# Which four experts a mixture-of-experts loop computes first, and its first and last step written out

## The chip, the cores and the metric

One core of one Trainium2 chip runs the whole program. The time is device microseconds (us) from the first to the last instruction and what lies around them, a median over runs; smaller is better.

## What is computed

One denoising step of a two-layer model on two samples of 128 tokens (sample 0 is the prompt, sample 1 the latent tokens), 1024 wide, float32. Each layer has a mixer and then a mixture of 32 experts. Only the second half of a layer matters here:

```python
g_idx = argmax(hf @ rg_w + rg_b)                     # one of 4 groups
top_v, top_i = top_k(e_logits of that group, 2)      # two of its 8 experts
w_sel = softmax(g_logits)[g_idx] * softmax(top_v)
hid = silu(einsum('nd,edf->nef', hf, w_gate)) * einsum('nd,edf->nef', hf, w_up)     # f = 256
out = einsum('nef,efd->nd', hid * gates, w_down)
```

The two samples make 512 picks of an expert in each layer, and the picks are uneven. Worked out from the reference's router and its inputs, the experts with picks are (expert: picks of sample 0 + picks of sample 1):

- layer 0: 0: 35+56, 1: 13+20, 2: 46+2, 3: 32+15, 4: 22+29, 5: 1+3, 6: 14+10, 7: 61+73, 8: 1+0, 9: 1+0, 24: 10+8, 25: 4+12, 26: 2+3, 27: 1+1, 28: 0+13, 29: 1+2, 30: 11+7, 31: 1+2
- layer 1: 8: 30+37, 9: 29+16, 10: 45+112, 11: 46+52, 12: 12+3, 13: 1+2, 14: 60+9, 15: 1+3, 16: 2+0, 17: 0+2, 18: 0+3, 19: 1+5, 20: 1+4, 24: 1+1, 25: 1+3, 26: 2+0, 27: 3+1, 28: 7+3, 30: 8+0, 31: 6+0

## The kernel before

An expert's picks are cut into chunks of 32 tokens. TensorE works on four columns of 32 at once, so one **step** of the expert loop computes four chunks, one in each column, and each column holds the weights of one expert: 6144 elements on each of 128 partitions, in three parts of 2048, the first and second half of the gate and up weights (`gu0`, `gu1`) and the down weights (`down`), 1024 KB each. A chunk plan made on the chip gives layer 0 seven steps (28 chunks) and layer 1 eight (32 chunks).

SyncE (SP) loads the weights into the columns, with one buffer for each column: in its own loop (L680 to L692) it reads the experts of the next step and a flag `fresh` for each column from the small table `meta`, waits until TensorE is done with the part (`gu0_done`, `gu1_done`, `down`), and issues the four loads of it; a column whose expert stays (`fresh` 0) moves nothing. The first step's weights are loaded earlier: as soon as sample 0 is routed, `first_keys`, `first_ranks` and `first_experts` on VectorE (DVE) rank the experts by the picks of sample 0 and take the **four least picked** (ranks 0 to 3 among those with a pick), and SP issues their twelve loads while sample 1 is still in its norm and router. Every chunk that is left then goes into the columns in the order of the experts, column after column, and `meta` is signalled when both samples are routed. In a step TensorE (PE) does, in this order:

- gate and up, `gu0` then `gu1` (L1282, 64 matmuls)
- the gather of the next step's tokens, as a product with a one-hot matrix (L1247)
- two times two transposes, of the gates (L1295) and of the hidden values (L1298)
- the scatter of the step before into four sums in PSUM (L1258); in step 0 it adds zeros
- down (L1310)

ScalarE (ACT) takes the exponential, copies `tH` and `tG`, and the first half of the output; DVE makes the hidden values (L2442 to L2448), the gates and the next selection. After the loop the last scatter follows (L1319). PE, ACT and DVE each wait for `meta` and read the number of steps before step 0. GpSimd (POOL) waits for the end of the down product of step 1 (`down` at 6, L781) and then loads the gate rows and norm weights for the end of the layer: two loads of 512 KB and one of 1024 KB, on the second DMA queue (q0), while SP's go through q1.

Of the kernel before, what the change touches and what calls it, by code (L numbers as in the profile page):

```python
# [15 lines left out]
ALU = mybir.AluOpType  # L16
# [3 lines left out]
P = 128  # L20
# [3 lines left out]
NS = 2  # L24
# [38 lines left out]
NCST = C_G4 + 64  # L63


def constants():
# [22 lines left out]
    c[:, C_M8:C_M8 + 8] = np.arange(8) - 1000.0  # L89
    return c  # L90
# [97 lines left out]
def build(nc, a, o):  # L188
# [41 lines left out]
    small = view(region(320), 320)  # L230
# [19 lines left out]
    BK2 = Banks(ps, [6], S("filled_side"), {"dve": S("drained_side")})  # L250
# [184 lines left out]
    def plan_first(l):  # L435
# [5 lines left out]
        for kind in ("first", "ranked", "early"):  # L441
            BK.add((kind, l), "dve")
# [3 lines left out]
    def plan_moe(l):  # L446
# [9 lines left out]
        for kind in ("base", "eid"):  # L456
            BK2.add((kind, l), "dve")
# [150 lines left out]
    R_EID, R_F, R_RF, R_F4 = 952, 1004, 1036, 1068  # L608
    R_FLAG, R_D = R_ZERO, R_ZERO + 64
# [24 lines left out]
    def _(sp):  # L634
# [26 lines left out]
        for l in range(2):  # L661
# [17 lines left out]
            steps = sp.value_load(meta[0:1, 0, 0:1], min_val=MINS, max_val=MAXT)  # L679
            with sp.Fori(1, steps) as it:  # L680
# [5 lines left out]
                for h in range(2):  # L686
                    sp.wait_ge(S(f"gu{h}_done{l}"), it + 1)
                    for c in range(NC):
                        load(f"gu{h}", *GU[h], c, expert[c], cond=fresh[c])
                sp.wait_ge(S(f"down{l}"), it * 2 + 2)  # L690
# [21 lines left out]
    def _(pool):  # L712
# [63 lines left out]
        for l in range(2):  # L776
# [4 lines left out]
            pool.wait_ge(S(f"down{l}"), 6)  # L781
# [20 lines left out]
    def _(pe):  # L802
# [376 lines left out]
        def first_rows(l):  # L1179
# [3 lines left out]
            pe.matmul(bank[0:1, 0:NC], cst[0:32, C_COL:C_COL + 1], rt_[0:32, R_F4:R_F4 + NC], start=True, stop=True)  # L1183
            pe.matmul(bank[:, 32:64], rt_[0:32, R_NB:R_NB + P], ident[0:32, 0:32], start=True, stop=True)
            pe.matmul(bank[:, 64:96], rt_[0:32, R_ZERO:R_ZERO + P], ident[0:32, 0:32], start=True, stop=True)\
                .then_inc(filled, 1)

# [10 lines left out]
        first_rows(0)  # L1198
        project_out(0, 1, 1, range(7, KT))


        def moe(l):
# [5 lines left out]
            filled_side = S("filled_side")  # L1208
            rows(l, 0)
# [20 lines left out]
            side_free("base")  # L1230
            pe.wait_ge(S("nchunks"), l + 1)
            bank, nb = side("base"), rt_[0:32, R_NB:R_NB + P]
            pe.matmul(bank[:, 0:32], nb, SU[0:32, 0:32], start=True, stop=True)
            pe.matmul(bank[:, 32:33], nb, ones[0:32, 0:1], start=True, stop=True)
            pe.matmul(bank[0:32, 64:65], UI[0:32, 0:32], nb[:, 0:1], start=True, stop=True).then_inc(filled_side, 1)
            for h in range(2):
                pe.sem_inc(S(f"gu{h}_done{l}"), 1)
            pe.sem_inc(S(f"down{l}"), 2)
# [3 lines left out]
            def gather(n, tiles=range(KT)):  # L1242

                pe.wait_ge(S(f"selected{l}"), n + 1)
                for k in tiles:
# [3 lines left out]
                    if k % 4 == 3:  # L1249
                        mm.then_inc(S(f"gathered{l}"), 1)  # L1250
# [1365 lines left out]
```

## Time and profile before

| | |
|---|---|
| median of 3 runs | 944.57 us (943.24 to 945.4) |
| the profiled execution | 940.24 us, span 938.4 us |
| granted TensorE clock, mean | 0.97 of full |
| PE / DVE / ACT busy | 845.4 (90%) / 493.0 (53%) / 192.3 (20%) us |
| DMA | 226.85 MB, mean 242 GB/s |
| expert loop, layer 0 and layer 1 | first gate and up at 422.13 and 757.83 us, last scatter at 567.62 and 919.99 us |

The profiled execution is 4.3 us below the median of the runs. A busy PE is not a PE at its peak. In the rows, an entry in brackets after a group is the time that its engine sat idle before it and what ended that.

### The profile page before, as it was taken

To read this page: it belongs to the slowest core of one execution; us is meant where nothing else is said; L and a number is where in the kernel's file an instruction comes from. 1 tells how busy PE (TensorE), PEld (TensorE's weight loads), DVE (VectorE), ACT (ScalarE), POOL (GpSimd) and SP (SyncE) were. 2 spreads that over 40 slices of the span, in tenths; PEclk is the share of its full clock that TensorE was granted. 3 is DMA by queue.
4 is the path that set the end of the run, shared out by engine and by line. 5 is a ranking of instruction groups with operands and counts; after the bars stand their busy time and mean duration, and the time that the engine had idled before them with its cause. 6 is when DMAs were issued, how large, how long until landed. Compare 5 with 4: busy or idle time off the path is not lost. (4 is left out here: it accounts for less than half of the span.)

```text
span 938.4 us, 14579 instructions
## 1 busy us (share of the span) xinstructions
PE 845.4 (90%) x5328; PEld 516.2 (55%) x5328; DVE 493.0 (53%) x1287; ACT 192.3 (20%) x538; POOL 41.9 (4%) x62
## 2 busy tenths in 40 slices
PE   3899989999999989989799978999879887999893
PEld 0687865777677675573345435444555752444351
DVE  1244589898864684675224426011375771432356
ACT  0125631222211211121111101110562210111110
POOL 1000140000000000000000001000000000000000
PEclk9999999999999999999899989999999998999997
DMA  9941269565454410099989785544100699989961
GB/s 366 411 181 68 90 253 415 194 264 184 153 213 181 186 38 34 20 409 421 418 322 413 282 373 203 216 179 159 66 1 1 262 422 421 373 344 404 420 262 45
DMA packets 29071, 226.85 MB, mean 242 GB/s; under 512 B 4105, under 2 KB 4521, under 8 KB 8033
## 3 DMA queue, kind: packets, MB, share of 16 engines
q1 hardware_dynamic: 25504, 214.57, 57.1%
q0 software_dynamic: 3520, 11.66, 3.7%
q8 instruction: 29, 0.48, 0.2%
q14 instruction: 18, 0.14, 0.0%
HBM read 286.74 MB, written 2.39 MB: 308 GB/s over the span
## 5 line engine op out<-in xcount | busy, mean ns | idle before, releaser
L1282 PE MATMUL ps<-arena 128*32 128x512 f32 x960 | 114.9, 628 | 25.6 <-DMA arena<-in_w_exp 23.6
L1282 PEld LDWEIGHTS ps<-arena 128*32 128x32 f32 x960 | 31.2, 115 | 105.7 <-issue 74.1
L1467 ACT ACTIVATE arena<-ps 128x256 f32<-128x256 f32 (+1 forms) x106 | 41.7, 435 | 212.8 <-PE ps L838 133.0
L1336 PE MATMUL ps<-arena 128*128 128x512 f32 x192 | 83.0, 592 | 0.8 <-ACT arena L1475 0.6
L922 PE MATMUL ps<-arena 128*128 128x256 f32 x368 | 81.6, 380 | 1.9 <-ACT arena L1475 1.9
L922 PEld LDWEIGHTS ps<-arena 128*128 128x128 f32 x368 | 69.0, 189 | 14.5 <-ACT arena L1475 2.1
L838 PE MATMUL ps<-arena 128*128 128x128 f32 x432 | 61.4, 278 | 14.2 <-DVE arena L2532 4.7
L1247 PEld LDWEIGHTS ps<-arena 128*128 128x128 f32 x544 | 63.0, 193 | 17.8 <-issue 10.9
L1247 PE MATMUL ps<-arena 128*128 128x128 f32 x544 | 66.6, 280 | 4.4 <-DVE arena L2348 4.4
L1029 PE MATMUL ps<-arena 128*128 128x192 f32 x320 | 65.3, 351 | 3.8 <-DVE arena L2070 1.6
L838 PEld LDWEIGHTS ps<-arena 128*128 128x128 f32 x432 | 48.4, 142 | 35.2 <-issue 10.3
L2442 DVE TENSOR_SCALAR arena<-arena 128x256 f32<-128x256 f32 x15 | 4.4, 296 | 119.1 <-ACT arena L1687 118.5
L1029 PEld LDWEIGHTS ps<-arena 128*128 128x128 f32 x320 | 55.2, 201 | 19.3 <-issue 11.5
L813 PE MATMUL ps<-arena 128*32 128x512 f32 x384 | 51.1, 636 | 15.0 <-DMA arena<-in_cst 13.0
L1336 PEld LDWEIGHTS ps<-arena 128*128 128x128 f32 x192 | 36.1, 189 | 46.4 <-issue 46.4
L1310 PE MATMUL ps<-arena 128*32 128x512 f32 x480 | 54.6, 595 | 0.0
L1258 PE MATMUL ps<-arena 128*128 128x512 f32 x120 | 54.0, 592 | 0.0
L2054 DVE SCALAR_TENSOR_TENSOR arena<-arena 128x256 f32<-128x256 f32 x120 | 52.4, 482 | 0.1
L2152 DVE COPY arena<-ps 128x256 f32<-128x256 f32 x80 | 33.9, 423 | 24.5 <-PE ps L1029 24.3
L2455 DVE COPY arena<-ps 128x512 f32<-128x512 f32 x15 | 10.4, 693 | 59.4 <-PE ps L1310 59.4
L1687 ACT ACTIVATE arena<-ps 128x256 f32<-128x256 f32 x15 | 5.8, 385 | 152.5 <-PE ps L1282 152.5
L1310 PEld LDWEIGHTS ps<-arena 128*32 128x32 f32 x480 | 13.9, 109 | 38.4 <-issue 38.4
(344 smaller groups left out, 1102.8 us busy)
## 6 DMA issues: line engine op xcount, KB each, us to landing
arena<-in_w_exp SPq DMA_DIRECT2D x180, 1024.0 KB
arena<-in_mod_w SPq DMA_DIRECT2D x24, 2048.0 KB, 7.7
arena<-in_od_in_w SPq DMA_DIRECT2D x6, 2048.0 KB, 7.6
arena<-in_ev_in_w SPq DMA_DIRECT2D x5, 2048.0 KB, 29.6
arena<-in_ev_out_w SPq DMA_DIRECT2D x2, 2048.0 KB, 7.5
arena<-gate_rows POOLq DMA_DIRECT2D x8, 512.0 KB, 9.0
arena<-in_ln POOLq DMA_DIRECT2D x4, 1024.0 KB, 11.5
arena<-in_od_out_w SPq DMA_DIRECT2D x2, 2048.0 KB, 7.6
```

The source lines that it names most:

```text
L813: mm = pe.matmul(bank[q:q + 32, :], cond[:, k, :], w[:, k, :], start=(k < 4), stop=(k >= 4), skip_group_check=True)
L838: mm = pe.transpose(bank[:, n * P:(n + 1) * P], t, ident)
L922: mm = pe.matmul(bank[:, n * 256:n * 256 + 256], slot(("evin", i // 4))[:, k, (i % 4) * P:(i % 4 + 1) * P], hT[:, k, :], start=(k == 0), s ...
L1029: mm = pe.matmul(BK.bank(key)[:, (i % 2) * 192:(i % 2) * 192 + 192], lt[i], now[:, i, :], start=True, stop=True)
L1247: mm = pe.matmul(ps[:, 4 + k // 4, (k % 4) * P:(k % 4 + 1) * P], hb[:, s, k * P:(k + 1) * P], sel[:, s, :], start=(s == 0), stop=(s == 1))
L1258: mm = pe.matmul(ps[:, 2 * s + half, :], tG[:, s * P:(s + 1) * P], ysb[:, half * 512:(half + 1) * 512], start=False, stop=False, skip_grou ...
L1282: mm = pe.matmul(ps[32 * c:32 * c + 32, 6, :], xg[:, k, 32 * c:32 * c + 32], EW[:, c, k * 512:(k + 1) * 512], start=(k == 0), stop=(k == K ...
L1310: mm = pe.matmul(ps[32 * c:32 * c + 32, 4 + half, :], tH[:, f * P + 32 * c:f * P + 32 * c + 32], w, start=(f == 0), stop=(f == 1), skip_gr ...
L1336: mm = pe.matmul(BK.bank(key), hT[:, k, s * T:(s + 1) * T], slot(("odin", c))[:, k, :], start=(k == 0), stop=(k == KT - 1))
L1467: BK.drained_by(A(out, take(key)[:, 0:n], ACT.Copy), key)
L2054: ins = STT(out, src, w, out, ALU.mult, ALU.add)
L2152: own.inc(V.tensor_copy(new[:, pair, 0:P], src[:, :, 0:P]))
```

## The change

First experts: the two **most** picked and the two least picked of sample 0. `C_PICK` holds three rows from which `first_ranks` makes the wanted ranks: with `used` experts picked, columns 0 to 3 take ranks `used-1`, `used-2`, 0 and 1. An expert of the first step keeps its column as long as it has chunks (up to the number of steps), and the other chunks fill the columns behind it in the order of the experts. This takes more work in the plan: a total first (`tot`), then positions (`base`), then the experts of each place (`eid`), and about twice the small operations on DVE. The number of chunks and of steps stays. The early part sends two rows for each expert through PE in a matmul of its own (`first_columns`).

The loop: step 0 and the last step stand outside it on PE, ACT and DVE. Step 0 no longer waits for `meta`, and has no scatter of zeros; the last step has no gather. Six warming matmuls before the first gather are gone, and the plan's small matmuls use PSUM bank 7. POOL's wait becomes `down` at 4, since the count of 2 that PE gave ahead of the loop is gone too: it is the same place, the end of step 1.

```diff
-        for kind in ("first", "ranked", "early"):
+        for kind in ("first", "ranked", "early", "frows"):
...
-            steps = sp.value_load(meta[0:1, 0, 0:1], min_val=MINS, max_val=MAXT)
+            steps = sp.value_load(meta[0:1, 0, 1:2], min_val=MINS, max_val=MAXT)
...
-                    sp.wait_ge(S(f"gu{h}_done{l}"), it + 1)
+                    sp.wait_ge(S(f"gu{h}_done{l}"), it)
...
-                sp.wait_ge(S(f"down{l}"), it * 2 + 2)
+                sp.wait_ge(S(f"down{l}"), it * 2)
...
-            pool.wait_ge(S(f"down{l}"), 6)
+            pool.wait_ge(S(f"down{l}"), 4)
...
+        def first_columns(l):
+            BK.wait_free(pe, ("frows", l))
+            pe.wait_ge(S("early_columns"), l + 1)
+            bank = BK.bank(("frows", l))
+            pe.matmul(bank[:, 0:64], ones[0:32, :], rt_[0:32, R_NB:R_NB + 64], start=True, stop=True).then_inc(filled, 1)
...
-            warm(6)
             gather(0, range(4))
+            side_free("base")
+            pe.wait_ge(S("based"), l + 1)
...
             gather(0, range(4, KT))
+            pe.wait_ge(S(f"xg_act{l}"), 1)
+            pe.wait_ge(S(f"xg_dve{l}"), 1)
+            for h in range(2):
+                pe.wait_ge(S(f"gu{h}_loaded{l}"), 64)
+                for k in range(4 * h, 4 * h + 4):
+                    gate_up(xg, k)
...
+            gather(1)
+            BK2.wait_drained(pe, ("eid", l))
+            pe.wait_ge(S(f"gates{l}"), 1)
+            turn(0)
+            pe.wait_ge(S(f"xg_act{l}"), 2)
+            pe.wait_ge(S(f"xg_dve{l}"), 2)
+            down(0)
             pe.wait_ge(S("cleared"), 4 * l + 4)
-            BK2.wait_drained(pe, ("eid", l))
             pe.wait_ge(S(f"meta{l}"), 1)
-            steps = pe.value_load(meta[0:1, 0, 0:1], min_val=MINS, max_val=MAXT)
+            last = pe.value_load(meta[0:1, 0, 0:1], min_val=MINS - 1, max_val=MAXS)
...
+            with pe.Fori(1, last) as n:
+                gate_ups(n)
...
+            gate_ups(last)
+            pe.wait_ge(S(f"y_read{l}"), last)
+            pe.wait_ge(S(f"y_read_dve{l}"), last)
+            pe.wait_ge(S(f"tG{l}"), last)
+            scatter(last - 1)
+            pe.wait_ge(S(f"gates{l}"), last + 1)
+            turn(last)
+            down(last)
...
+                own.link(STT(want, pick(0), col(39), pick(1), ALU.mult, ALU.add))
+                own.link(TT(want, want, pick(2), ALU.max))
+                sig(TS(F4[:, 0:NC], want, col(36), None, ALU.is_equal), "early_rows")
...
+            own.link(STT(col(34), col(33), sc[0:32, 48:49], col(37), ALU.min, ALU.mult))
...
+            sig(V.memset(sc[:, 62:64], 0.0), f"meta{l}")
...
+            gates(0, 6, place)
+            hidden(0)
+            gathered(1)
+            step_end(0)
+            out_half(0)
```

PE around step 0 of layer 0, before: the second half of gather 0 (L1247), then the wait for `meta0` (L1274), then the loop, of which L1282 is gate and up.

```order
L1247 MATMUL ps<-arena 128x128 [waits selected0]
L1247 MATMUL ps<-arena 128x128 x7
L1267 MATMUL ps<-arena 1x48 [waits ended,drained_side]
L1247 MATMUL ps<-arena 128x128 [waits selected0]
L1247 MATMUL ps<-arena 128x128 x7
L1274 TENSOR_LOAD meta [waits meta0,drained_side,cleared]
L1274 ISA x2
L1275 UNCONDITIONAL_BRANCH
L1275 ISA
L1279 ISA [waits xg_dve0,xg_act0]
L1282 MATMUL ps<-arena 32x512 [waits gu0_loaded0]
L1282 MATMUL ps<-arena 32x512 x15
```

After: `base` (L1294 to L1296) stands between the halves of gather 0 (L1230), and gate and up of step 0 (L1219) follow it without `meta0`.

```order
L1294 MATMUL ps<-arena 128x72 [waits based,drained_side]
L1295 MATMUL ps<-arena 128x1
L1296 MATMUL ps<-arena 32x1
L1230 MATMUL ps<-arena 128x128 [waits selected0]
L1230 MATMUL ps<-arena 128x128 x7
L1219 MATMUL ps<-arena 32x512 [waits gu0_loaded0,xg_dve0,xg_act0]
L1219 MATMUL ps<-arena 32x512 x15
L1307 MATMUL ps<-arena 1x48 [waits ended,drained_side]
L1219 MATMUL ps<-arena 32x512 [waits gu1_loaded0]
L1219 MATMUL ps<-arena 32x512 x15
L1230 MATMUL ps<-arena 128x128 [waits selected0]
L1230 MATMUL ps<-arena 128x128 x15
```

What moved is the wait for `meta0`: it now stands behind the down product of step 0.

PE in the second half of a step and behind the loop, before: gather (L1247), transposes, scatter (L1258), down (L1310), last scatter (L1319 follows).

```order
L1247 MATMUL ps<-arena 128x128 x15
L1295 MATMUL ps<-arena 128x128 [waits tG0,gates0]
L1295 MATMUL ps<-arena 128x128
L1298 MATMUL ps<-arena 128x128 [waits hid0]
L1298 MATMUL ps<-arena 128x128
L1258 MATMUL ps<-arena 128x512 [waits y_read_dve0,y_read0]
L1258 MATMUL ps<-arena 128x512 x3
L1310 MATMUL ps<-arena 32x512 [waits xg_dve0,down_loaded0,xg_act0,tH0]
L1310 MATMUL ps<-arena 32x512 x15
```

After, the last step of layer 0: gate and up (L1219), scatter (L1258), transposes (L1237, L1240), down (L1250).

```order
L1219 MATMUL ps<-arena 32x512 [waits gu1_loaded0]
L1219 MATMUL ps<-arena 32x512 x15
L1258 MATMUL ps<-arena 128x512 [waits tG0,y_read_dve0,y_read0]
L1258 MATMUL ps<-arena 128x512 x3
L1347 REGISTER_ALU
L1237 MATMUL ps<-arena 128x128 [waits gates0]
L1237 MATMUL ps<-arena 128x128
L1240 MATMUL ps<-arena 128x128 [waits hid0]
L1240 MATMUL ps<-arena 128x128
L1250 MATMUL ps<-arena 32x512 [waits down_loaded0,tH0]
L1250 MATMUL ps<-arena 32x512 x15
```

The gather is gone there, and the scatter stands before the transposes, so that nothing lies between them and the down product.

DVE at the signal of `meta0`, before: it comes ahead of the copy of the gathered tokens of step 0 (L2357).

```order
L2389 TENSOR_SCALAR arena<-arena 1x1 [waits drained_side]
L2390 CAST meta<-arena 1x1 [waits dve_steps]
L2391 TENSOR_SCALAR arena<-ps 1x48 [waits filled_side]
L2392 CAST meta<-arena 1x48 [waits drained_side]
L2393 TENSOR_TENSOR arena<-arena 1x48
L2394 CAST meta<-arena 1x48 [waits dve_steps]
L2395 MEMSET arena 128x2 [waits dve_steps]
L2357 COPY arena<-ps 128x512 [waits gathered0,meta0]
```

After: the copy for step 0 has come before (L2404 now), then 31 operations that give the positions, four that make the selection for step 1, and then these.

```order
L2530 TENSOR_TENSOR arena<-arena 1x48 [waits selected0,dve_loop0]
L2531 TENSOR_SCALAR arena<-arena 1x1
L2532 CAST meta<-arena 1x1 [waits dve_steps]
L2533 CAST meta<-arena 1x1
L2534 TENSOR_SCALAR arena<-ps 1x48 [waits filled_side]
L2536 TENSOR_TENSOR arena<-arena 1x48 [waits dve_steps,drained_side]
L2537 TENSOR_TENSOR arena<-arena 1x48 [waits dve_steps]
L2538 TENSOR_TENSOR arena<-arena 1x48 [waits dve_steps]
L2539 CAST meta<-arena 1x48 [waits dve_steps]
L2540 TENSOR_TENSOR arena<-arena 1x48
L2541 CAST meta<-arena 1x48 [waits dve_steps]
L2542 MEMSET arena 128x2 [waits dve_steps]
```

The signal of `meta0` (at L2542's memset) now stands behind the selection for step 1.

## Rows read from the trace of the kernel before

**Rows 1.** The page: the span of the profiled execution.
```profile
span 938.4 us, 14579 instructions
```

**Rows 2.** Timeline of TensorE, layer 0, steps 0 to 2: start, length (us), line.
```profile
422.13 7.09 PE L1282 MATMUL ps<-arena 128*32 128x512 f32 x64 [1.04 <-DVE arena L2357]
430.92 3.84 PE L1247 MATMUL ps<-arena 128*128 128x128 f32 x32 [1.70 <-DVE arena L2348]
...
438.56 3.64 PE L1310 MATMUL ps<-arena 128*32 128x512 f32 x32
442.02 3.62 PE L1282 MATMUL ps<-arena 128*32 128x512 f32 x32
451.21 5.68 PE L1282 MATMUL ps<-arena 128*32 128x512 f32 x32 [5.57 <-DMA arena<-in_w_exp]
...
467.93 7.07 PE L1282 MATMUL ps<-arena 128*32 128x512 f32 x64
```

**Rows 3.** The same for steps 4 to 6 and the end of layer 0.
```profile
504.13 3.62 PE L1282 MATMUL ps<-arena 128*32 128x512 f32 x32
508.88 3.65 PE L1282 MATMUL ps<-arena 128*32 128x512 f32 x32 [1.13 <-DMA arena<-in_w_exp]
...
523.56 7.06 PE L1282 MATMUL ps<-arena 128*32 128x512 f32 x64
...
541.65 3.62 PE L1282 MATMUL ps<-arena 128*32 128x512 f32 x32
551.38 5.10 PE L1282 MATMUL ps<-arena 128*32 128x512 f32 x32 [6.10 <-DMA arena<-in_w_exp]
556.40 3.84 PE L1247 MATMUL ps<-arena 128*128 128x128 f32 x32
...
564.05 3.64 PE L1310 MATMUL ps<-arena 128*32 128x512 f32 x32
567.62 3.70 PE L1319 MATMUL ps<-arena 128*128 128x512 f32 x8
```

**Rows 4.** The same in layer 1: the second halves that waited.
```profile
788.25 6.12 PE L1282 MATMUL ps<-arena 128*32 128x512 f32 x32 [6.29 <-DMA arena<-in_w_exp]
...
846.23 3.65 PE L1282 MATMUL ps<-arena 128*32 128x512 f32 x32 [1.02 <-DMA arena<-in_w_exp]
...
885.42 5.33 PE L1282 MATMUL ps<-arena 128*32 128x512 f32 x32 [2.80 <-DMA arena<-in_w_exp]
```

**Rows 5.** Window: PE and PEld busy, granted clock, DMA share, GB/s.
```profile
451.21:456.89 5.68, 5.68 (x32) 1.23 (x32) 0.63 1.02 424
```

**Rows 6.** Timeline of SyncE's issues, three windows.
```profile
397.92 33.75 SPq L667 DMA_DIRECT2D arena<-in_w_exp  x20
...
442.50 2.17 SPq L667 DMA_DIRECT2D arena<-in_w_exp  x4
...
448.24 1.69 SPq L667 DMA_DIRECT2D arena<-in_w_exp  x4
```

**Rows 7.** DMA queues, 468 to 486 us (packets, MB, share), and POOL times.
```profile
q1 hardware_dynamic: 657, 4.77, 67.2%
q0 software_dynamic: 432, 2.10, 28.0%
...
468.68 1.04 POOL L765 DMA_DIRECT2D arena<-gate_rows  x2 [94.28 <-PE ps L1310]
```

**Rows 8.** Timeline of VectorE around step 0 of layer 0 (last row: layer 1).
```profile
419.94 0.06 DVE L2395 MEMSET arena<- 128x2 f32 x1
421.19 0.69 DVE L2357 COPY arena<-ps 128x512 f32<-128x512 f32 x1 [1.19 <-PE ps L1247]
...
422.96 0.23 DVE L2404 TENSOR_TENSOR arena<-arena 128x64 f32<-128x64 f32 x1
...
431.49 1.75 DVE L2444 RECIPROCAL arena<-arena 128x256 f32<-128x256 f32 x1
...
755.65 0.06 DVE L2395 MEMSET arena<- 128x2 f32 x1
```

## The prediction on record

> **What bounds the kernel now.** I read the page first for the span [rows 1], then the timeline of TensorE through both expert loops. Where no weights are late, a step repeats every 18.1 us, back to back (467.93, and two steps later 504.13) [rows 2, 3]: the matmuls bound it. The steps that lose time wait ahead of the second half of gate and up, for a DMA: 5.57 us in step 1, 1.13 in step 4 and 6.10 in step 6 of layer 0 [rows 2, 3]; 6.29, 1.02 and 2.80 us in steps 1, 4 and 6 of layer 1 [rows 4]. The six waits are 22.9 us. The four long ones cost more: the half takes 5.68, 5.10, 6.12 and 5.33 us instead of 3.6 behind a wait of 2.8 us or more, and 3.65 behind 1.0 to 1.1 us. In the first of them the granted clock was 0.63, so partly at its 1.2 GHz level and partly at 2.4 [rows 5].
>
> The waits follow from the fresh experts. Laying the picks out by the rule of the kernel before gives, step by step, 4 4 2 1 3 1 4 fresh columns in layer 0 and 4 4 2 1 3 2 3 2 in layer 1; the waits are in just the steps with 4 or 3. One part of an expert (1.05 MB) at 420 to 424 GB/s takes 2.5 us [rows 5]. The second half of step 6 starts 27.8 us after step 5 has begun (551.38 less 523.56), that of a step with 3 fresh 4.75 us earlier in its own period (508.88 less 504.13 plus 18.1, 22.8 us); these differ by 5 us, two parts. It is wanted at 18.1 + 3.5 = 21.6 us. So 2 fresh (17.9 us) never wait, 3 are 1.1 us late, 4 are 6.2 us late.
>
> **The change, part by part.** The same layout by the new rule (a most picked expert keeps its column) gives 4 2 2 3 2 4 2 in layer 0 and 4 2 2 3 3 2 3 2 in layer 1. The loads are 19 and 21 experts, as before: the change moves no byte less, it moves loads to later steps.
>
> *Ahead of the loop.* On VectorE an operation on 64 columns that waits for the one before costs 0.26 us (422.96 to the next start; 0.23 busy) [rows 8], a small one 0.2, one that doesn't wait 0.1. `first_columns` waits for six more operations of VectorE, about 1.0 us, of which 0.5 us reaches the path through the rest of the output projection (in layer 1 0.6). I take 0.5. The first selection is about 0.7 us earlier, and the three matmuls of `base` between the gather's halves, 0.7 us, take that back. Gate and up of step 0 stays at about 422.6 in layer 0.
>
> *Step 1.* `meta` moves behind the copy at 421.19 and 47 operations, 28 waiting at 0.24 us on average and 19 at 0.1, 8.7 us. With the copy's 0.6 and the 0.5 from above it is signalled at 431.0, not at 420.0 [rows 8]. SyncE then needs 3.6 us for its registers before the first issue (from 444.67, where four issues end, to 448.24) [rows 6], and skips two columns: first fresh issue at 435.4. From there four parts (10.0 us) and 2.7 us of start and landing follow. The same sum before: first issue 397.92 [rows 6], 20 parts 50.0 us, 451.21 less these is 3.3 us. So the second half can start at 448.1, 3.1 us earlier than 451.21. The tensor engine's own path is just shorter: hidden values at 436.6 (five operations for the gate weights, five for the gates, then 3 us with the reciprocal of 1.75 us [rows 8]), copy of `tH` 0.9, down 3.5, a register read of 0.6: step 1 begins at 442.1, against 442.02 [rows 2]. The scatter that is gone (3.6 us) is eaten by that wait. The slow clock cost 2.1 us of this half before (5.68 for 3.6); I allow 1 us for it after, so step 1 ends 4.2 us earlier in layer 0. In layer 1 `meta` came at 755.7 [rows 8]; 11.0 + 3.6 + 0.8 + 12.7 us later is 783.8, 4.4 us before 788.25, and of the 2.5 us of slow clock there (6.12) [rows 4] 1.5 goes: 5.9 us.
>
> *Step 3.* Here the change pays. POOL's three loads are issued as step 1 ends (468.68, down ended at 467.9) and move 2.10 MB in the next 18 us: 28.0% of 18 us is 5.0 us of all DMA engines [rows 7]. Before, the next steps had 2 and 1 fresh, and this was hidden. Now step 3 has 3. From the start T of step 2, the down parts of step 2 (5.0 us), six parts of step 3 (15.0) and POOL's 5.0 stand in line from T + 1.7, and land 1.75 later: T + 28.4, wanted at T + 21.6. That is 6.8 us late, and for the clock, between 0 and 1.7 by [rows 4], I take 1.2: 8.0 us in each layer, 16.0 together. Bounds: 1.1 us a layer if POOL's loads stood aside, 10 if the clock falls twice.
>
> What the row shows is that both queues were busy at once, with 67.2 and 28.0% of the time [rows 7]. The Trainium skill says why ("DMA: Bandwidth & Descriptors", Queues, rings and completion order): each DMA engine goes round robin between the queue rows that have work. By that rule the collision cannot be avoided by the queue, and the trace agrees; if the queues were apart, the sum would be 13.8 us lower.
>
> *Step 4.* Layer 0: 2 fresh instead of 3, 1.1 us saved [rows 3]. Layer 1: 3 fresh behind 3; nine parts (22.5 us) between the two landings against 18.1 of compute and 1.2 of clock, 3.2 late, less 1.0 before [rows 4]: 2.2 lost.
>
> *Steps 5 and 6.* The four fresh of layer 0 move from step 6 to 5, with the same 6.1 us of wait. Layer 1 keeps its three in step 6. 0 us.
>
> *Last step.* Gate and up ends at 556.4, down starts at 564.05 [rows 3], 7.65 us. Now the scatter (3.6 us) covers the hidden values, then transposes 0.4 and the copy of `tH`, which nothing hides any more, 0.8: 4.8 us. 2.8 us saved, twice: 5.6. In the other peeled step the wait for weights takes the gain, as above.
>
> Sum: -4.2 - 5.9 + 16.0 - 1.1 + 2.2 - 5.6 = **+1.4 us**. The profiled execution took 940.24 us, 1.8 of them outside its span [rows 1], and the median is 944.57, 0.46% above it; so 941.6 for a profile like it, and **946.0** for the median. I call 0.2% (1.9 us) what a measurement of this kernel can tell from no change.
>
> **Rivals.**
> *POOL's loads cost nothing.* The engines could give SyncE's queue the larger part while it is full, with POOL's loads in the gaps. For it: in [rows 7] q0 has under half the share of q1. Against it: they moved all of their 2.10 MB in this very stretch, and the engines were busy 95% of it. Then steps 3 are 1.1 us late: 946.0 - 13.8 = 932, and about 1 less for layer 1's step 4. Faster. It decides from some 3.5 us of wait a layer downward. Chance 0.12.
>
> *The clock falls in step 0 as well.* Six warming matmuls are gone, and by the times above PE has gaps of about 2.5 us before the first gather and before the transposes of the hidden values. For it: 1.0 us of idle time was followed by no loss and 2.8 us by 1.7 [rows 4]. Against it: what is lost before the second half of step 1 is partly hidden by the wait there. If a fall costs 2.5 us a layer in full: 951. Slower. Chance 0.14.
>
> *The chain to `meta` is longer than I made it.* From the count of picks on it has 81 operations of VectorE in place of 33; each microsecond goes straight into step 1, in both layers. At 0.06 us more for each of the 47 it is 2.8 us a layer: 951 as well. Chance 0.06, with the one above 0.20.
>
> *The loads do not move as laid out* (a tie in the ranks, another number of steps). The layout of before fits every wait in the trace, so 0.02.
>
> **How the numbers follow.** The sum as worked out has 0.66: its own range is 941.5 to 950.5, from the clock terms (0 to 3.4 us a stall) and 1 us either way in each POOL collision; of it 0.14 is faster by over 0.2%, 0.27 within it, 0.25 slower. The first rival is faster (0.12). The next two are slower, but for 0.03 that the range of the sum swallows (0.17 and 0.03). The last is split. Together: faster 0.27, same 0.31, slower 0.42. The range leaves out the far end of the first rival and what lies over two clock falls: 937 to 952.5.
>
> **What would show it.** In the timeline of TensorE, the wait ahead of the second half of step 1 falls from 5.6 and 6.3 us to 2 or less, and a new wait of some 6 to 7 us, in one or two pieces, stands in step 3 of both layers, with POOL's issues one step ahead of it. In layer 0 the wait of 6 us is in step 5 and none in step 6; in layer 1 step 4 waits about 3 us. The last step takes 2.8 us less from gate and up to the last scatter. The DMA moves as many bytes as before. It is wrong if step 3 waits under 3 us, if `meta` comes before 429 or after 433 in layer 0, or if the halves behind short waits take 5 us and more.

## The result, and the profile after

The changed kernel took **952.87 us** (median of 4 runs, 951.54 to 956.7); the kernel before took 943.9 beside it (4 runs). The ratio is 1.0104, with an interval of 1.0081 to 1.0126. On another chip, with more runs behind it, it was 1.0161 (1.0119 to 1.0203). So it is slower by 1.0 to 1.6%, against a forecast of 1.0015 (946.0 us) and a range that ended at 952.5, just under the measured median.

The profiled execution is 16.4 us longer than the one of before [rows 1]. The page gives its span:

```profile
span 954.8 us, 14276 instructions
```

The timeline of TensorE in layer 0 (start, length, line; in brackets the idle time before a group and what ended it). L1173 is the matmul that ranks the first experts, L1230 the gather, L1219 gate and up, L1250 down, L1258 and L1355 the scatter:

```profile
394.46 0.20 PE L1173 MATMUL ps<-arena 128*32 128x1 f32 x2 [0.53 <-DVE arena L2309]
...
418.58 3.75 PE L1230 MATMUL ps<-arena 128*128 128x128 f32 x16 [2.64 <-DVE arena L2395]
423.40 3.78 PE L1230 MATMUL ps<-arena 128*128 128x128 f32 x16
428.01 3.65 PE L1219 MATMUL ps<-arena 128*32 128x512 f32 x32 [0.83 <-issue]
...
443.33 6.12 PE L1250 MATMUL ps<-arena 128*32 128x512 f32 x32 [0.68 <-ACT arena L1724]
...
454.73 3.65 PE L1219 MATMUL ps<-arena 128*32 128x512 f32 x32 [1.84 <-DMA arena<-in_w_exp]
...
469.41 7.06 PE L1219 MATMUL ps<-arena 128*32 128x512 f32 x64
...
491.34 3.65 PE L1219 MATMUL ps<-arena 128*32 128x512 f32 x32 [3.65 <-DMA arena<-in_w_exp]
498.79 5.34 PE L1219 MATMUL ps<-arena 128*32 128x512 f32 x32 [3.81 <-DMA arena<-in_w_exp]
...
515.16 7.06 PE L1219 MATMUL ps<-arena 128*32 128x512 f32 x64
...
535.51 3.65 PE L1219 MATMUL ps<-arena 128*32 128x512 f32 x32 [2.07 <-DMA arena<-in_w_exp]
545.44 6.26 PE L1219 MATMUL ps<-arena 128*32 128x512 f32 x32 [6.29 <-DMA arena<-in_w_exp]
...
562.73 7.06 PE L1219 MATMUL ps<-arena 128*32 128x512 f32 x64
569.72 3.70 PE L1258 MATMUL ps<-arena 128*128 128x512 f32 x8
...
577.91 3.70 PE L1355 MATMUL ps<-arena 128*128 128x512 f32 x8
```

The waits stand where they were laid out: a short one in step 1, a new one of 7.5 us in two pieces in step 3, the one for 4 fresh in step 5 (8.4 us, in two pieces) and none in step 6. But the two halves of the first gather take 3.75 and 3.78 us, where before they took 2.89 and 2.05, and the down of step 0 takes 6.12 for 3.64. The same view of layer 1:

```profile
738.29 0.20 PE L1173 MATMUL ps<-arena 128*32 128x1 f32 x2 [0.19 <-DVE arena L2309]
...
762.73 3.49 PE L1230 MATMUL ps<-arena 128*128 128x128 f32 x16 [2.58 <-DVE arena L2395]
...
790.25 3.65 PE L1219 MATMUL ps<-arena 128*32 128x512 f32 x32 [1.84 <-DMA arena<-in_w_exp]
796.67 5.24 PE L1219 MATMUL ps<-arena 128*32 128x512 f32 x32 [2.78 <-DMA arena<-in_w_exp]
...
812.95 7.06 PE L1219 MATMUL ps<-arena 128*32 128x512 f32 x64
...
834.83 4.94 PE L1219 MATMUL ps<-arena 128*32 128x512 f32 x32 [3.61 <-DMA arena<-in_w_exp]
842.29 3.65 PE L1219 MATMUL ps<-arena 128*32 128x512 f32 x32 [2.52 <-DMA arena<-in_w_exp]
...
857.21 3.65 PE L1219 MATMUL ps<-arena 128*32 128x512 f32 x32
864.66 5.34 PE L1219 MATMUL ps<-arena 128*32 128x512 f32 x32 [3.80 <-DMA arena<-in_w_exp]
...
881.03 7.06 PE L1219 MATMUL ps<-arena 128*32 128x512 f32 x64
...
904.82 5.34 PE L1219 MATMUL ps<-arena 128*32 128x512 f32 x32 [2.07 <-DMA arena<-in_w_exp]
...
936.37 3.70 PE L1355 MATMUL ps<-arena 128*128 128x512 f32 x8
```

To subtract stage by stage, six more rows of the kernel before are needed, the ranking in both layers, the starts of three steps of layer 1 and its last scatter:

```profile
392.05 0.20 PE L1171 MATMUL ps<-arena 128*32 128x1 f32 x2 [0.54 <-DVE arena L2266]
...
728.11 0.20 PE L1171 MATMUL ps<-arena 128*32 128x1 f32 x2 [0.20 <-DVE arena L2266]
...
805.40 7.06 PE L1282 MATMUL ps<-arena 128*32 128x512 f32 x64
...
841.59 3.62 PE L1282 MATMUL ps<-arena 128*32 128x512 f32 x32
...
860.91 7.06 PE L1282 MATMUL ps<-arena 128*32 128x512 f32 x64
...
919.99 3.70 PE L1319 MATMUL ps<-arena 128*128 128x512 f32 x8
```

From the ranking to the start of step 2 (469.41 and 812.95; before 467.93 [rows 2] and 805.40) the change gains 0.9 us in layer 0 and 2.6 in layer 1. Steps 2 and 3 together lose 9.6 us (45.75 for 36.20) and 8.1 (44.26 for 36.19). Layer 0's steps 4 to 6, to the last scatter, gain 0.7; by pieces that is 1.3 gained in step 4, 3.6 lost in steps 5 and 6 and 3.0 gained in the last. Layer 1's step 4 loses 4.5 us, and its steps 5 to 7 gain 3.7, of which 3.0 are in the last. The sum, before rounding, is +14.1 us. The remaining 2.4 us lie ahead of the ranking in layer 0 (394.46 less 392.05), in code that the change doesn't touch. They are a difference between executions: in the profile of g2, which is the changed kernel once more, the ranking stands at 389.14. Its two expert stages, each from the ranking to the last scatter, are 11.5 us longer than before, in place of 14.1.

### The profile page after: what moved, and what is told of

Same layout as the page of the kernel before. It is cut to its first block and busy times, and to the rows that moved or that the text cites. A ratio compares the mean times of both kernels' runs of the same rounds, so it can differ in the third digit from the quotient of the medians.

```text
span 954.8 us, 14276 instructions
## 1 busy us (share of the span) xinstructions
PE 843.4 (88%) x5224; PEld 510.4 (53%) x5224; DVE 489.9 (51%) x1317; ACT 191.0 (20%) x536; POOL 41.9 (4%) x62
## 5 line engine op out<-in xcount | busy, mean ns | idle before, releaser
L1219 PE MATMUL ps<-arena 128*32 128x512 f32 x960 | 118.5, 642 | 36.0 <-DMA arena<-in_w_exp 34.3
L1219 PEld LDWEIGHTS ps<-arena 128*32 128x32 f32 x960 | 31.7, 117 | 118.4 <-issue 73.0
L1372 PE MATMUL ps<-arena 128*128 128x512 f32 x192 | 83.0, 592 | 0.8 <-ACT arena L1512 0.6
L924 PEld LDWEIGHTS ps<-arena 128*128 128x128 f32 x368 | 69.0, 189 | 14.5 <-ACT arena L1512 2.1
L840 PE MATMUL ps<-arena 128*128 128x128 f32 x432 | 62.5, 281 | 14.2 <-DVE arena L2639 4.7
L840 PEld LDWEIGHTS ps<-arena 128*128 128x128 f32 x432 | 49.5, 144 | 35.7 <-issue 10.7
L1230 PEld LDWEIGHTS ps<-arena 128*128 128x128 f32 x480 | 59.6, 205 | 16.3 <-issue 16.3
L1230 PE MATMUL ps<-arena 128*128 128x128 f32 x480 | 63.0, 292 | 5.2 <-DVE arena L2395 5.2
L1031 PE MATMUL ps<-arena 128*128 128x192 f32 x320 | 63.3, 344 | 3.0 <-DVE arena L2113 1.1
L815 PE MATMUL ps<-arena 128*32 128x512 f32 x384 | 51.1, 636 | 15.0 <-DMA arena<-in_cst 13.0
L1031 PEld LDWEIGHTS ps<-arena 128*128 128x128 f32 x320 | 53.6, 196 | 18.5 <-issue 10.6
L1372 PEld LDWEIGHTS ps<-arena 128*128 128x128 f32 x192 | 36.1, 189 | 46.4 <-issue 46.4
L1250 PE MATMUL ps<-arena 128*32 128x512 f32 x480 | 57.1, 617 | 2.3 <-ACT arena L1724 2.3
L1258 PE MATMUL ps<-arena 128*128 128x512 f32 x104 | 47.0, 594 | 0.0
L1250 PEld LDWEIGHTS ps<-arena 128*32 128x32 f32 x480 | 14.7, 112 | 40.5 <-issue 39.1
```

What stands on the lines that cost most here:

```text
L815: mm = pe.matmul(bank[q:q + 32, :], cond[:, k, :], w[:, k, :], start=(k < 4), stop=(k >= 4), skip_group_check=True)
L840: mm = pe.transpose(bank[:, n * P:(n + 1) * P], t, ident)
L924: mm = pe.matmul(bank[:, n * 256:n * 256 + 256], slot(("evin", i // 4))[:, k, (i % 4) * P:(i % 4 + 1) * P], hT[:, k, :], start=(k == 0), s ...
L1031: mm = pe.matmul(BK.bank(key)[:, (i % 2) * 192:(i % 2) * 192 + 192], lt[i], now[:, i, :], start=True, stop=True)
L1219: mm = pe.matmul(ps[32 * c:32 * c + 32, 6, :], xs[:, k, 32 * c:32 * c + 32], EW[:, c, k * 512:(k + 1) * 512], start=(k == 0), stop=(k == K ...
L1230: mm = pe.matmul(ps[:, 4 + k // 4, (k % 4) * P:(k % 4 + 1) * P], hb[:, s, k * P:(k + 1) * P], sel[:, s, :], start=(s == 0), stop=(s == 1))
```

## The experiments

Ten kernels ran, and the changed one once more (g2). Each ratio is to the kernel before on the same chip, with its 95% interval; the changed kernel stands at 1.0104 and 1.0161. The e runs, the f runs and the g runs were on three different chips, and g2 stands beside g1 and g3 only; so a ratio of an e or f run is compared with the changed kernel's across chips, with both of its figures.

| kernel | median us | ratio | interval |
|---|---|---|---|
| e1: POOL's loads as the last step begins | 947.48 | 1.0071 | 1.0043 to 1.0099 |
| f1: POOL's loads inside the last step | 941.06 | 1.0016 | 0.9987 to 1.0045 |
| e2: kernel before, POOL's loads a step later | 954.12 | 1.0156 | 1.0112 to 1.0199 |
| e3: four least first | 951.37 | 1.0117 | 1.0074 to 1.0161 |
| e4: warming matmuls | 947.82 | 1.0083 | 1.0046 to 1.012 |
| f2: meta early | 940.37 | 1.0009 | 0.9984 to 1.0035 |
| f3: f1, f2 and e4 together | 926.53 | 0.986 | 0.983 to 0.989 |
| g3: f3 without warming | 933.12 | 0.9905 | 0.9869 to 0.994 |
| g1: f3 with the four least first | 943.77 | 1.0045 | 1.0016 to 1.0074 |
| f4: kernel before, last step peeled | 936.96 | 0.9973 | 0.9949 to 0.9996 |
| g2: the changed kernel again | 955.28 | 1.0161 | 1.0119 to 1.0203 |

**POOL's loads, moved (e1, then f1).**

```diff
-            pool.wait_ge(S(f"down{l}"), 4)
+            pool.wait_ge(S(f"down{l}"), (12, 14)[l])        # e1
+            pool.wait_ge(S(f"gu0_done{l}"), (7, 8)[l])      # f1
```

> The changed kernel, with POOL's three loads (2.1 MB) issued when the step before the last has ended, where nothing fresh is to be loaded, in both layers. Theory (collision): the 5.0 us of all DMA engines that they take leave step 3. What stays there is 3 fresh behind a step of 2 fresh, which waited 2.8 us and cost 1.7 us of clock in layer 1 of the kernel before: step 3 falls from 27.7 and 25.9 us to about 22.6, so 8 to 9 us less in all, about 944. Rival 1 (POOL's loads cost nothing, the fresh parts alone make the wait): no change, 953. Rival 2 (POOL's loads are the whole wait, as the prediction's sum had it): 14 us less, 939. Step 5 of layer 0: if its 8.4 us of wait are left over from step 3 they fall to 6; if they come from the two down parts that stand ahead, they stay at 8.4.

> The changed kernel, with POOL's three loads issued when the first half of gate and up of the last step is done, so behind the last down parts. In the run before, with the loads issued at the end of the step before the last, the down of the last step came 2.6 us late with 1.7 of clock in layer 0 and 1.5 us late in layer 1. Theory (the loads only moved their collision there): these 4.3 and 1.5 us go too, step 3 stays at 18 to 22 us in place of 27.7 and 25.9: a ratio to the kernel before of 1.000 to 1.003, against 1.0104 of the changed kernel and 1.0071 of that run. Rival (a part of it is the clock, which falls elsewhere): 1.005 to 1.007.

The timeline of TensorE in e1, steps 3 and 6 of layer 0:

```profile
493.06 3.65 PE L1219 MATMUL ps<-arena 128*32 128x512 f32 x32 [1.91 <-DMA arena<-in_w_exp]
...
567.74 5.34 PE L1250 MATMUL ps<-arena 128*32 128x512 f32 x32 [3.07 <-DMA arena<-in_w_exp]
```

The 7.5 us of wait in step 3 are down to 1.91 here. But the loads met the down parts of the last step, which are issued at the same moment: a new wait of 3.07 us and 1.7 of slow clock in layer 0, and one of 1.98 us in layer 1. That is why e1 gave back only a part: 3 us by the first figure of the changed kernel and 8 to 9 by the second, where 8 to 9 were expected. The same rows of f1, with POOL's loads issued at 555.19:

```profile
490.59 3.65 PE L1219 MATMUL ps<-arena 128*32 128x512 f32 x32 [1.51 <-DMA arena<-in_w_exp]
...
524.03 3.65 PE L1219 MATMUL ps<-arena 128*32 128x512 f32 x32 [0.48 <-DMA arena<-in_w_exp]
533.97 6.00 PE L1219 MATMUL ps<-arena 128*32 128x512 f32 x32 [6.30 <-DMA arena<-in_w_exp]
...
563.02 3.64 PE L1250 MATMUL ps<-arena 128*32 128x512 f32 x32 [0.47 <-ACT arena L1724]
```

Now the wait ahead of down is gone too, and the kernel is level with the one before, inside the expected 1.000 to 1.003. The three loads cost 8 to 14 us where the change put them (1.0104 or 1.0161, less 1.0016). Step 5 of layer 0 still waits 6.8 us in all. It waits 7.3 in e1 and 8.4 in the changed kernel, but 7.3 in g2, which is the changed kernel too; so nothing left over from step 3 is shown in it.

The profiles of all kernels with the new choice say the same as this pair. With POOL's loads where the change put them (the changed kernel, g2, e4, f2), steps 2 and 3 of layer 0 take 43.9 to 45.8 us and steps 2 to 4 of layer 1 67.9 to 68.1. With the loads in the last step (e1, f1, f3, g3) they take 37.9 to 39.2 and 61.3 to 62.6. The means differ by 6.1 and 6.4 us.

**The same collision, made in the kernel before (e2).**

```diff
-            pool.wait_ge(S(f"down{l}"), 6)
+            pool.wait_ge(S(f"down{l}"), 8)
```

> The kernel before, with POOL's three loads issued one step later, so that they meet the loads of step 4 (3 fresh) in place of step 3 (1 fresh), in both layers. Collision theory: one down part, six parts of step 4 and POOL's 5.0 us stand in line, which lands 4 to 5 us after the half is wanted in place of 1.1, and the clock takes 1 to 2 more: 5 us a layer, 10 in all, about 954. Rival (POOL's loads give way): no change, 944.

The second halves of step 4 in layers 0 and 1 of e2:

```profile
513.44 5.34 PE L1282 MATMUL ps<-arena 128*32 128x512 f32 x32 [3.80 <-DMA arena<-in_w_exp]
...
859.18 5.34 PE L1282 MATMUL ps<-arena 128*32 128x512 f32 x32 [3.81 <-DMA arena<-in_w_exp]
```

Before, they waited 1.13 and 1.02 us [rows 3, 4]. With the 0.6 and 0.5 us that the first halves wait now and 1.7 of clock each, step 4 is 5.2 us longer in both layers. By its ratio the kernel is 15 us slower (its interval begins at 10.5), where these steps show the expected 10; one number in one wait made the kernel before as slow as the changed one. The rest of the difference between the two profiles lies outside step 4, mostly between the layers, where the same stretch takes 160 to 164 us from one execution to another.

**The first experts alone (e3).**

```diff
-    c[:, C_PICK:C_PICK + 12] = [1, 1, 0, 0, -1, -2, 0, 1, 3, 2, 0, 1]
+    c[:, C_PICK:C_PICK + 12] = [0, 0, 0, 0, 0, 1, 2, 3, 0, 1, 2, 3]
```

> The changed kernel with the four least picked experts first, as in the kernel before; the code is otherwise that of the changed kernel, so meta stays late and the first and last steps stay peeled. Fresh columns are again 4 4 2 1 3 1 4 and 4 4 2 1 3 2 3 2. Theory: step 1 now has to load 8 parts behind the late meta, four more: its second half starts 8 to 10 us later in each layer (wait about 10 us in place of 1.8 and 2.8), +18; step 3 loses its wait (-9.6 and -7.8), step 4 returns to 19.4 and 19.3 us (+1.3 and -4.8), the 4 fresh stand in step 6 behind 1 fresh (-3.6, +0.7). Sum about -6: 947. Rival (the late meta costs nothing, since step 0 starts later too): step 1 as in the kernel before, 936 to 938.

The two halves of step 1, layer 0, in e3:

```profile
447.97 5.95 PE L1219 MATMUL ps<-arena 128*32 128x512 f32 x32 [4.49 <-DMA arena<-in_w_exp]
458.94 5.59 PE L1219 MATMUL ps<-arena 128*32 128x512 f32 x32 [5.02 <-DMA arena<-in_w_exp]
```

Behind the late meta four fresh columns wait 9.5 us (11.2 in layer 1), where two wait 1.8 (4.6). Step 3 waits no more. The two effects about cancel: 1.0117 against 1.0104 and 1.0161. So the new choice did what it is for in step 1, and it was paid for in step 3. My sum of -6 leaned to a gain; the ratio can't tell it from no change against the first figure, and is 4 us faster, with intervals that overlap, against the second.

**Clock in step 0 (e4).** Nine warming matmuls go ahead of the first gather, eight ahead of the transposes of the hidden values:

```diff
                     pe.transpose(ps[:, 7, (2 + s) * P:(3 + s) * P], gsel[:, 0, s, :], ident)
+                warm(fill)
                 pe.wait_ge(S(f"hid{l}"), n + 1)
...
+            warm(9, 6)
             gather(0, range(4))
...
-            turn(0)
+            turn(0, 8)
```

> The changed kernel with warming matmuls in the two places where TensorE now stands still in the head: 9 ahead of the first gather and 8 ahead of the transposes of the hidden values, both layers. Clock theory: the low clock over the gathers (3.75 and 3.78 us for 2.05 in layer 0, 3.49 in layer 1) and over down of step 0 (6.12 for 3.64) goes, of which the waits of 1.8 us in step 1 give back a part: 2 to 5 us less, 948 to 951. Rival (the wait for weights in step 1 absorbs it, or the clock falls anyway): within 1 us of the changed kernel.

Windows of layer 0 from the first gather to gate and up (busy time of PE, PEld, DVE, ACT, POOL, granted clock, DMA share, GB/s). First the changed kernel:

```profile
418.58:428.01 9.43, 8.60 (x38) 8.08 (x39) 3.40 (x19) 0.60 (x1) 0.00 (x0) 0.51 1.01 420
```

then e4:

```profile
420.24:425.78 5.54, 4.71 (x39) 4.40 (x40) 3.46 (x19) 0.60 (x1) 0.00 (x0) 1.00 1.02 421
```

In the changed kernel the granted clock was 0.51, so at its 1.2 GHz level, behind 2.64 us in which TensorE stood still; with matmuls there it stayed at 2.4 GHz, and the stretch is 3.9 us shorter. How long the clock stays low differs between executions of the same code: in e1, f1, f2 and g3, without warming, the first half of the gather takes the same 3.75 us, but the second runs at full speed (2.05), and the stretch is 1.8 to 2.0 us shorter than the 9.43 above. But step 1 gave the down's 2.5 us back: its halves waited 1.84 and 2.66 us for their weights in place of 0 and 1.84, and from gate and up of step 0 to the end of step 1 it was 30.4 us for 30.3.

What warming is worth in the head as a whole, from the ranking to the start of step 2, two more pairs of rows of e4 show:

```profile
396.22 0.20 PE L1173 MATMUL ps<-arena 128*32 128x1 f32 x2 [0.53 <-DVE arena L2311]
...
467.30 7.06 PE L1219 MATMUL ps<-arena 128*32 128x512 f32 x64
...
734.35 0.20 PE L1173 MATMUL ps<-arena 128*32 128x1 f32 x2 [0.19 <-DVE arena L2311]
...
805.75 7.06 PE L1219 MATMUL ps<-arena 128*32 128x512 f32 x64
```

That is 71.1 and 71.4 us, where the four profiles with the same head and no warming (the changed kernel, g2, e1, f1) have 73.8 to 75.5 and 74.3 to 74.7: 3.5 and 3.0 us less than their means. The ratio moved by 0.2% against the first measurement and by 0.8% against the second, so 2 or 7 us where 2 to 5 were expected; the intervals overlap both times, the second time only just, so the time of the whole kernel alone doesn't show the gain.

**The chain to meta (f2).** The matmul for the experts moves behind the first gather, and VectorE's last twelve operations for meta move behind the first copy of gathered tokens, ahead of the places of the later steps:

```diff
             gather(0, range(4, KT))
+            side_free("eid")
+            pe.wait_ge(S("ended"), l + 1)
+            pe.matmul(side("eid")[0:1, 0:NC * MAXS], ...).then_inc(filled_side, 1)
...
             gathered(0)
+            eid, flag = ...
+            ...
+            sig(V.memset(sc[:, 62:64], 0.0), f"meta{l}")
             own.inc(TS(sc[:, 52:55], ...))
```

> The changed kernel with the chain to meta put ahead: the matmul for the experts of the steps behind the first gather in place of between the halves of gate and up, and VectorE's operations for meta straight behind the copy of the first gathered half, ahead of the places of the later steps. meta comes about 6 us earlier, the places of step 1 about 2 us later. Theory (step 1 is bound by the late meta through SyncE): the waits of step 1 (1.84 us in layer 0; 1.84 and 2.78 with 1.6 of clock in layer 1) go, 2 and 6 us less, and nothing else changes: ratio 1.0104 less 0.006 to 0.009, 1.002 to 1.005. Rival (TensorE's own chain over the gathers and the hidden values bounds step 1, or the second gather is now late for its selection): within 0.002 of 1.0104.

The timeline of VectorE has the signal of meta in layer 0 of the changed kernel, and that of SyncE the issues behind it:

```profile
436.44 0.06 DVE L2542 MEMSET arena<- 128x2 f32 x1
```

```profile
440.34 3.66 SPq L669 DMA_DIRECT2D arena<-in_w_exp  x8
```

In f2 the signal stands at

```profile
429.39 0.06 DVE L2500 MEMSET arena<- 128x2 f32 x1
```

and the timeline of TensorE at step 1 is

```profile
446.14 7.09 PE L1219 MATMUL ps<-arena 128*32 128x512 f32 x64
```

Counted from the first gather, meta comes after 9.3 us in place of 17.9, and gate and up of step 1 runs through (7.09 us, no wait). The slow down of step 0 was gone as well (3.64 us), though nothing warmed it. The kernel came 9 to 14 us back to 1.0009, more than the expected 1.002 to 1.005. The expectation had 2 and 6 us; from gate and up of step 0 to step 2 the profile shows 36.6 us in both layers for 41.4 and 43.2, so 4.8 and 6.6.

**All three together (f3), and without warming (g3).**

> The changed kernel with POOL's loads in the last step, the early chain to meta and the warming matmuls ahead of the first gather and of the transposes of step 0. Theory: the three add up (-8 to -9, -6 to -8, and -3 to -5 us, as without the wait of step 1 nothing hides the clock any more): ratio 0.989 to 0.995, faster than the kernel before. Rival (they fix the same microseconds twice): 0.997 to 1.002.

> The kernel with POOL's loads in the last step and the early chain to meta, without the warming matmuls. Theory (they gained only 2 us alone because the wait of step 1 took the rest back, and with that wait gone the whole of the clock's price shows): 3 to 5 us slower than the kernel with all three, ratio 0.989 to 0.991. Rival (two microseconds, as alone): 0.988.

Ratio 0.986: 13 us faster than the kernel before and 23 to 28 faster than the changed kernel, and beyond the expected 0.989 to 0.995. The gains add up: 2.4 or 3.0% together, 2.0 or 3.8% as the sum of the three alone, by the first and the second measurement of the changed kernel. Without the warming it is 0.9905, as expected, so by the ratios warming is worth 4 us here. That is not shown, though: the intervals overlap a little (up to 0.989 and from 0.9869), the two kernels ran on different chips, and their profiled executions are level (spans of 924.1 and 924.0 us). In them the head is 0.8 and 1.5 us shorter with warming, and the steps behind it give that back.

**Is the new choice worth something then (g1)?**

> The kernel with all three mends (POOL's loads in the last step, early chain to meta, warming matmuls), but with the four least picked experts first. Theory (with the mends the choice of the first experts is worth what it saves in step 1): 8 parts from the first issue (about 7 us after step 0 began in the mended kernel) need 20 us and 4.6 of start and landing, so step 1 waits about 8 us and loses 1.5 to 2 to the clock in each layer; step 3 saves the 2.8 and 2.3 us that it waits in the mended kernel, layer 1's step 4 some 4.5, step 6 about 1. Sum +8 to +10: ratio 0.994 to 0.997. Rival (the choice is worth nothing, all of the mended kernel's gain is in the mends): 0.984 to 0.988.

1.0045 against 0.986, 17 us, and well above the expected 0.994 to 0.997. Not all of it is step 1 (a wait of 6.93 us and 1.5 of clock in layer 0). With 4 fresh columns in the last step, POOL's loads stand in the way of its down parts. The timeline of g1 there:

```profile
566.41 5.34 PE L1251 MATMUL ps<-arena 128*32 128x512 f32 x32 [4.47 <-DMA arena<-in_w_exp]
```

In the last step down usually starts 4.6 us after the scatter ahead of it, here 8.6, and lasts 1.7 longer: 5.7 us that the placement costs and not the choice, and that the expectation had not counted. That leaves some 12 us for the choice by the ratios. By the profiled executions it is 9.5: the two stages are 15.2 us longer than in f3, less the same 5.7. This is the worth of the choice behind the peeled step 0 with its later `meta`. No run has the new choice with the first step and the plan as they were, or the peeled step 0 without the rest, so what these two are worth alone stays open.

**The last step peeled, alone (f4).**

```diff
-            with pe.Fori(0, steps) as n:
+            with pe.Fori(0, last) as n:
...
+            gate_up(last)
...
+            scatter(last - 1).then_inc(S(f"scattered{l}"), 1)
...
+            turn(last)
+            down(last)
```

> The kernel before with its last step alone peeled: no gather for a step that isn't there, and the scatter of the step before ahead of the transposes, so that it covers the hidden values. First experts, first step, chain to meta and POOL's loads are those of the kernel before. Theory: 2.8 to 3.0 us a layer from the last gate and up to the last scatter (11.2 to 8.2 us), about 6 us in all: ratio 0.993 to 0.995. Rival (the clock falls in the shorter step, or the 6 us of wait for the weights in step 6 of layer 0 absorbs it): 0.997 to 1.000.

0.9973 (2.5 us) lies in the range of the rival, 0.997 to 1.000, and the rival's second reason is what the rows show. The timeline of f4, end of layer 0:

```profile
549.60 6.22 PE L1283 MATMUL ps<-arena 128*32 128x512 f32 x32 [7.45 <-DMA arena<-in_w_exp]
555.75 3.71 PE L1258 MATMUL ps<-arena 128*128 128x512 f32 x8
...
563.94 3.70 PE L1332 MATMUL ps<-arena 128*128 128x512 f32 x8
```

From the end of gate and up to the last scatter it takes 8.2 us, as in the changed kernel, for 11.2 before. But the wait ahead of it is 7.45 us for 6.10 [rows 3], and the half takes 6.22 for 5.10, so layer 0 keeps 0.6 of 3.0 us. Layer 1 keeps its 3.0 (15.2 us for 18.2 from the last gate and up to the last scatter). Why four fresh columns land 1.3 us later there (7.33 in e3 as well) stays open.

**The changed kernel again (g2).**

> The changed kernel as it is, once more, on the chip of the other runs: for a ratio with more runs behind it. It was 1.0104, interval 1.0081 to 1.0126; the same is expected. If it comes out under 1.008, the steps found in the profiled executions (14 us in the two expert stages) are larger than what a typical run pays, because the clock falls less often there.

1.0161, not below 1.008 but above the first figure. The two intervals overlap only from 1.0119 to 1.0126, and the 14.1 us of the first pair of profiles (1.5%) lie between the figures; with g2's own profile the two stages give 11.5 us (1.2%).

## Why the prediction was wrong

Its steps in its order, predicted and then measured, in us:

| step | predicted | profile |
|---|---|---|
| step 1 and all ahead of it | -4.2, -5.9 | -0.9, -2.6 |
| step 3 | +8.0, +8.0 | +9.6, +8.1 |
| step 4 | -1.1, +2.2 | -1.3, +4.5 |
| steps 5 and 6 | 0 | +3.6, -0.7 |
| last step | -2.8, -2.8 | -3.0, -3.0 |
| sum (before rounding) | +1.4 | +14.1 |

- **Step 1 is the step that failed**, with half of the miss (6.6 us of 12.7). The gain was there in kind: the wait fell from 5.57 to 1.84 us in layer 0. What was missing is the clock ahead of it. The prediction wrote that gate and up of step 0 "stays at about 422.6"; with the 2.4 us by which everything was later that is 425.0, and it came at 428.01. The gathers ran at 0.51 of the clock, and `meta`, which waits for their copy, was signalled at 436.44, 3.0 us later than 431.0 and 2.4. The 2.5 us that the down of step 0 lost were covered by the wait behind it. That the clock is the cause e4 shows: with it kept up, the head gains 4.8 and 5.9 us on the kernel before (71.1 for 75.9, 71.4 for 77.3), where the prediction had 4.2 and 5.9. The second rival named just this (the clock falls in step 0 as well, 951) and had 0.14. It argued that the wait of step 1 hides a part; that is so for the down, but what the gathers lose is not hidden, because `meta` waits for them too.
- **A second term of step 1 was too small, and others made up for it.** From the first issue behind `meta` to the second half it took 14.4 and 14.6 us, not 12.7. The prediction allowed 2.7 us beside the four parts, though its own row of before gives 3.3 (a stream of twenty parts [rows 6]); here 4.4 to 4.6 us stand beside them. Against that, the registers and skipped columns took 3.9 us and not 4.4, and layer 0's second half ran at full clock (3.65), where 1 us was allowed.
- **The count of VectorE's operations was right.** In e4, where the clock stays up, meta comes 32.1 us after the first issue of the layer; before it was 22.0 (419.94 less 397.92 [rows 6, 8]). That is 10.1 later (10.0 in layer 1), for 11.0 predicted. The third rival, a longer chain, is out.
- **Step 3 and POOL's loads were right in mechanism and about in size.** The first rival, that they cost nothing, is refuted from both sides: f1 takes the loads away from there, and steps 2 and 3 shorten by 7.9 and 3.7 us (37.90 and 40.58) and layer 1's step 4 by 3.1 (20.67), together 14.7; e2 makes the same collision in the kernel before. The prediction had 13.8, and the means over four profiles each give 12.5. The Trainium skill's rule ("DMA: Bandwidth & Descriptors", Queues, rings and completion order) is that a DMA engine goes round robin between the queues that have work. The trace agrees so far that both queues move data in the same 18 us; in which order an engine serves them it doesn't show. The DMA queues of the changed kernel from 470 to 488 us (packets, MB, share), SyncE's and POOL's:

```profile
q1 hardware_dynamic: 603, 4.43, 63.6%
q0 software_dynamic: 432, 2.10, 28.7%
```

- **Step 4 in layer 1 was under-sized** (2.2 for 4.5), and its queue was not the error: nine parts (22.5 us) were laid out between the two landings, and from one second half to the next it is 22.4 (842.29 to 864.66). Against them stood 18.1 us of compute and 1.2 of slow clock in step 3's second half. That half ran at full clock (3.65; the low clock had fallen on the half ahead, 4.94), so the wait was longer by as much, and step 4's own half then ran slow (5.34), for which nothing was allowed. In f1 it is the other way round: step 3's second half takes 5.34, and step 4 waits 2.4 us and runs at full clock. In f3, also without POOL's loads there, step 3's half takes 3.65 and step 4 waits 3.80 again. So how much shows in step 3 and how much in step 4 goes with the clock; only their sum goes with POOL's loads.
- **"Steps 5 and 6: 0" was wrong in layer 0.** I moved the 6.1 us with the four fresh columns. But ahead of them now stand the down parts of a step with 2 fresh, not 1. The step waits 2.07 and 6.29 us, and the half lasts 6.26 for 5.10. Over the eight profiles with this layout the wait is 6.8 to 8.4 us, and where POOL's loads stood makes no clear difference (7.3 to 8.4 with them in step 3, 6.8 to 8.0 without). Why a whole extra part of 2.5 us shows as 0.7 to 2.3 stays open.
- **The last step** was right, to 0.2 us in each layer.
- **Two of its signs of being wrong came up.** `meta` came after 433 in layer 0 (436.44), which points at the term that failed. And a half behind a short wait took over 5 us: 5.34 behind 2.07 in step 6 of layer 1. The prediction had the low clock begin behind 2.8 us; yet in step 3 of layer 0 a half behind 3.65 us ran at full clock (3.65). The length of the wait just ahead doesn't settle it.

The range fell short because the clock in the head was priced as a rival (5 us in all) and left out of the sum, while e4 shows 6.5 us of it: the gap ahead of the first gather acts twice, on TensorE's own path and through the copy that `meta` waits for. The rest of the miss, some 6 us, is in the steps behind: 1.7 in step 3, 2.1 in step 4 and 2.9 in steps 5 and 6, less 0.4 in the last.

## What to carry to other kernels

When loads move to other steps, lay the whole queue out anew, every other queue's loads with it: a wait constant of a third engine (here POOL's) was worth 8 to 14 us, and a single number in it made the kernel before as slow as the changed one. When a chain is lengthened that TensorE waits for, price the idle time at the clock as well, since what the gap costs is paid in the matmuls behind it. A result that many engines wait for (`meta`) belongs ahead of work that only the next step needs: twelve operations and one matmul moved up gave back 9 to 14 us, about all that the change had lost.

## What was not expected of the hardware

- 2.64 us without a matmul on TensorE ahead of the gathers were followed by 9.4 us at a granted clock of 0.51; in e4, with 18 warming matmul records (2.25 us) in that place, the clock stayed at 1.00. In four other executions of the same head (e1, f1, f2, g3) only the first 4.6 us or so were slow. In the kernel before a gap of 1.70 us in the same stage [rows 2] cost nothing that the next gather shows (3.84 us). But a gap is not the only thing that matters: in e2, with the head of the kernel before, the first half of the gather took 3.78 us behind a gap of 0.62.
- A queue that has run empty needed 4.6 us beside its four parts of 2.5 (14.6 in all, layer 1) from the first issue to the start of the second half, where a stream of twenty parts had 3.3 [rows 6]. What the difference of about 1 us is was not tried; some of it can be the rounding of a part to 2.5 us, taken twenty times.
- Between one second half that waits and the next, nine parts took 22.4 us in the changed kernel, in f1 and in f3, whether the compute between ran at full clock or not. So a half that runs slow shortens the next wait.
